# Turning the non-rotary queries of a latent attention on VectorE instead of TensorE, and moving the score products three tiles later

## The reference, cut to what matters

```python
q = (rms_norm(c_q, norm_cq) @ w_uq).reshape(B, S, MLA_HEADS, QK_NOPE + QK_ROPE)     # 128 + 64
q = jnp.concatenate([q[..., :QK_NOPE], apply_rope(q[..., QK_NOPE:], cos, sin)], axis=-1)
kv = (rms_norm(c_kv, norm_ckv) @ w_ukv).reshape(B, S, MLA_HEADS, QK_NOPE + V_HEAD)
...
s = jnp.einsum('bqhd,bkhd->bhqk', q[:, q0:kend], k[:, :kend]).astype(jnp.float32) * scale
p = jax.nn.softmax(jnp.where(mask, s, NEG_INF), axis=-1).astype(v.dtype)
outs.append(jnp.einsum('bhqk,bkhd->bqhd', p, v[:, :kend]))
```

## Time and profile before

| | |
|---|---|
| three runs | 1658.45 (median), 1657.43, 1869.51 us |
| the profiled execution | 1656.32 us, its span 1654.5 us |
| PE busy | 1645.2 us, 99% |
| DVE busy | 1156.0 us, 70% |
| ACT busy | 818.3 us, 49% |
| loads from HBM | 306.89 MB, 187 GB/s over the span |

### The profile page before, as it was taken

How to read it: one execution, slowest core, us unless ns; L and a number is a source line. 1 busy time by engine, 2 the same in 40 slices (tenths; PEclk the granted TensorE clock), 3 DMA queues, 4 the chain that set the end, 5 groups by cost and what they waited for, 6 DMA issues and landing times.

```text
span 1654.5 us, 23302 instructions
## 1 busy us (share of the span) xinstructions
PE 1645.2 (99%) x7752; PEld 1377.5 (83%) x7752; DVE 1156.0 (70%) x1528; ACT 818.3 (49%) x1044; POOL 109.7 (7%) x154
## 2 busy tenths in 40 slices
PE   9999999999999999999999999999999999999998
PEld 8888888888888888888888888888888888888886
DVE  5678877778988777885568766666666666654454
ACT  7556545555544544555555544444444444344343
POOL 3100111120000000120001100000000000000000
PEclk9999999999999999999999999999999999999999
DMA  7875655556566675554446666666666666565564
GB/s 238 250 205 171 181 163 146 167 160 186 162 190 204 199 231 169 200 196 155 145 132 193 198 193 196 195 190 192 192 194 183 190 203 194 195 219 180 186 211 137
DMA packets 161404, 309.81 MB, mean 187 GB/s; under 512 B 10272, under 2 KB 16928, under 8 KB 161088
## 3 DMA queue, kind: packets, MB, share of 16 engines
q1 hardware_dynamic: 159152, 302.03, 59.6%
q0 software_dynamic: 1488, 6.42, 1.1%
q10 hardware_dynamic: 704, 0.58, 0.1%
HBM read 306.89 MB, written 2.10 MB: 187 GB/s over the span
## 4 chain that ended last, share of the span: by engine, by line
PE 98%; ACT 1%; issue 1%; DMA 0%; DVE 0%; POOL 0%; POOLq 0%; ACTq 0%; SPq 0%; DVEq 0%
PE acc L374 30%; PE acc L376 30%; PE acc L375 30%; PE tp L386 1%; PE sc L527 1%; PE acc L603 1%; PE acc L605 1%; PE acc L604 1%; PE ov L508 0%; PE sc L522 0%; PE sc L497 0%; DMA raw<-in_w_in_dram 0%; PE ov L404 0%; PE acc L574 0%; PE acc L585 0%
## 5 line engine op out<-in xcount | busy, mean ns | idle before, releaser
L1339 DVE TENSOR_TENSOR w_lo<-raw,w_hi 128x1024 fp32r<-128x1024 f32 (+3 forms) x591 | 719.1, 1222 | 382.9 <-ACT w_hi L821 375.2
L821 ACT ACTIVATE w_hi<-raw 128x1024 fp32r<-128x1024 f32 (+3 forms) x591 | 605.7, 1027 | 753.8 <-PE acc L376 722.9
L374 PE MATMUL acc<-w_hi,crossT 128*128 128x512 f32 x832 | 324.8, 390 | 0.1
L375 PE MATMUL acc<-w_lo,crossT 128*128 128x512 f32 x832 | 323.9, 389 | 0.0
L376 PE MATMUL acc<-w_hi,crossT 128*128 128x512 f32 x832 | 323.9, 389 | 0.0
L374 PE MATMUL acc<-w_hi,mixT 128*128 128x512 f32 x732 | 289.1, 395 | 0.2
L376 PE MATMUL acc<-w_hi,mixT 128*128 128x512 f32 x732 | 285.2, 390 | 0.0
L375 PE MATMUL acc<-w_lo,mixT 128*128 128x512 f32 x732 | 285.1, 389 | 0.0
L374 PEld LDWEIGHTS acc<-w_hi,crossT 128*128 128x128 f32 x832 | 156.2, 188 | 33.0 <-ACTq L1072 0.5
L376 PEld LDWEIGHTS acc<-w_hi,crossT 128*128 128x128 f32 x832 | 156.2, 188 | 32.6
L375 PEld LDWEIGHTS acc<-w_lo,crossT 128*128 128x128 f32 x832 | 156.2, 188 | 31.9
(11 more groups left out here) (286 smaller groups left out, 1581.6 us busy)
## 6 DMA issues: line engine op xcount, KB each, us to landing
raw<-in_w_in_dram SPq DMA_DIRECT2D x104, 512.0 KB, 3.9
raw<-in_w_gate_dram SPq DMA_DIRECT2D x88, 512.0 KB, 3.9
raw<-in_w_up_dram SPq DMA_DIRECT2D x88, 512.0 KB, 3.7
raw<-in_w_down_dram SPq DMA_DIRECT2D x80, 512.0 KB, 4.6
raw<-in_w_kv_mem_dram SPq DMA_DIRECT2D x64, 512.0 KB, 3.7
raw<-in_w_o_dram SPq DMA_DIRECT2D x32, 512.0 KB, 4.4
raw<-in_w_q_mem_dram SPq DMA_DIRECT2D x32, 512.0 KB, 4.0
raw<-in_w_o_mem_dram SPq DMA_DIRECT2D x32, 512.0 KB, 4.1
```

The lines of the kernel that those rows point to most:

```text
L374: mm(o, lo, whi, start=first and k == 0, stop=False)
L375: mm(o, hi, wlo, start=False, stop=False)
L821: fn(w_hi[:, s, 0:width], raw[:, s, 0:width], ACT.Copy).then_inc(hi_done, 1)
L1339: V.tensor_tensor(w_lo[:, s, 0:width], raw[:, s, 0:width], w_hi[:, s, 0:width].bitcast(F32), ALU.subtract).then_inc(lo_done, 1)
```

## The change

The four transposes of the non-rotary queries leave PE. DVE does them as 16 instructions (`query_turn`), each of which transposes 32 x 32 squares of a 32-row band: for row band i and column band j the squares of both token blocks and both heads, 32 x 128 numbers. They stand between taps: squares 0 to 2 and 3 to 6 in steps 10 and 11 of the pair itself, 7 to 9, 10 to 12 and 13 to 15 in steps 0, 1 and 2 of the next pair (after the last pair: of the memory stage). DVE writes `qnT` itself, so ACT's copy of it goes. The two rotary transposes stay, now each in a bank of its own with its own copy on ACT. Values and scores on PE move from behind tile 3 to behind tile 6, masked scores on DVE from step 3 to 6, exponentials on ACT from step 4 to 7, the inverse of the row sums from step 7 to 8. The taps are shared out anew.

```diff
-            def queries_turned(p, q):
-
-                pe.wait_ge(q_ready, 2 * p + 2)
-                turn_group(q, 0, [q_tok[:, b, h, 0:NOPE] for h in range(2) for b in range(NB)])
+            def rotary_turned(p, q):
+
                 pe.wait_ge(rope_ready, p + 1)
-                turn_group(q, 1, [qr_tok[:, b, :, :].rearrange("p h d -> p (h d)") for b in range(NB)])
+                for b in range(NB):
+                    turn_group(q, b, [qr_tok[:, b, :, :].rearrange("p h d -> p (h d)")])
...
                 operand_ready(q)
+                pe.wait_ge(q_turned, p + 1)
                 pe.wait_ge(kv_ready, 2 * p + 2)
...
-                    queries_turned(i - 1, i + (Q_C - 1))
+                    rotary_turned(i - 1, i + (Q_C - 1))
                     if nth > 1:
                         probs_turn(i - 2)
-                if t == 3:
+                if t == 6:
                     if nth > 1:
                         values(i - 2, v_pair[parity], nth == 2)
                     scores(i - 1, i + (Q_C - 1), nth == 1)
...
-                fn(qnT[:, :, :].rearrange("p h t -> p (h t)"), tp[:, 0, :], ACT.Copy).then_inc(turned_out[0], 1)
-                act.wait_ge(turned, 2 * q + 2)
-                fn(qrT[:, :], tp[:, 1, 0:TOK], ACT.Copy).then_inc(turned_out[1], 1)
+                for b in range(NB):
+                    act.wait_ge(turned, 2 * q + (b + 1))
+                    fn(qrT[:, b * P:(b + 1) * P], tp[:, b, 0:P], ACT.Copy).then_inc(turned_out[b], 1)
...
-                if t == 4:
+                if t == 7:
                     exponentials(i - 1)
...
                         if not first:
-                            act.wait_ge(turned, 2 * i + (2 * Q_C - 1))
+                            act.wait_ge(q_turned, i)
                             act.wait_ge(rope_ready, i)
...
+            def query_turn(n):
+
+                i, j = n // 4, n % 4
+                src = q_tok[32 * i:32 * i + 32, :, :, 32 * j:32 * j + 32]
+                to = qnT[32 * j:32 * j + 32, :, :].rearrange("p h (b t) -> p b h t", b=NB)
+                ins = V.transpose(to[:, :, :, 32 * i:32 * i + 32], src)
+                if n == 15:
+                    ins.then_inc(q_turned, 1)
...
                     ins.then_inc(conv_step, 1)
+                    if turns:
+                        query_turn(turns.pop(0))
+                for n in turns:
+                    query_turn(n)
...
-                if t == 3:
+                if t == 6:
                     masked_scores(i - 1, nth == 1)
                 if t == 7:
                     if nth > 1:
                         gate_values(i - 2)
+                if t == 8:
                     row_inverse(i - 1, nth == 1)
...
-            share = [0, 0, 2, 3, 4, 6, 8, 10, 12, 14, 16, 18, EARLY_TAPS]
+            share = [0, 1, 3, 5, 8, 10, 12, 12, 13, 16, 18, 19, EARLY_TAPS]
...
-            share_last = [0, 3, 6, 7, 9, 12, 15, 18, 18, 18, 19, 19, EARLY_TAPS]
+            share_last = [0, 1, 3, 5, 9, 12, 15, 15, 16, 17, 18, 19, EARLY_TAPS]
+            turn_now = {0: (7, 10), 1: (10, 13), 2: (13, 16)}
+            turn_next = {10: (0, 3), 11: (3, 7)}
...
+                    turns = range(*turn_next.get(t, (0, 0)) if first or t > 9 else turn_now.get(t, (0, 0)))
+                    if t == 10:
+                        dve.wait_ge(q_ready, 2 * i + 2)
+                        if not first:
+                            dve.wait_ge(scores_ready, 2 * i)
...
-                late_taps(0, t, (0, 0, 1, 3, 6, 10, 14, 18, 22))
+                late_taps(0, t, (0, 1, 3, 5, 8, 12, 16, 18, 22), range(*turn_now.get(t, (0, 0))))
             for t in range(8):
                 split_lo(T_E + 8, t + 4)
+                if t == 0:
+                    row_inverse(PAIRS - 1, False)
```

More of the change, by code:

```diff
@@ L231, in program @@
         g_ready, u_turned, u_ready, tanh_done = (sem(n) for n in ("g_ready", "u_turned", "u_ready", "tanh_done"))
-        q_ready, kv_ready = sem("q_ready"), sem("kv_ready")
+        q_ready, q_turned, kv_ready = sem("q_ready"), sem("q_turned"), sem("kv_ready")
         rope_step, rope_ready = sem("rope_step"), sem("rope_ready")
@@ L965, in _, with rotary_out @@
                             fn(sqT[:, 2 * g:2 * g + 2, :], mem_k[:, 2 * g:2 * g + 2, :], ACT.Square).then_inc(sq_done, 1)
-            def queries_out(p, q, first):
-                act.wait_ge(turned, 2 * q + 1)
+            def rotary_out(p, q, first):
                 if not first:
                     act.wait_ge(scores_ready, 2 * p)
-                fn(qnT[:, :, :].rearrange("p h t -> p (h t)"), tp[:, 0, :], ACT.Copy).then_inc(turned_out[0], 1)
-                act.wait_ge(turned, 2 * q + 2)
-                fn(qrT[:, :], tp[:, 1, 0:TOK], ACT.Copy).then_inc(turned_out[1], 1)
+                for b in range(NB):
+                    act.wait_ge(turned, 2 * q + (b + 1))
+                    fn(qrT[:, b * P:(b + 1) * P], tp[:, b, 0:P], ACT.Copy).then_inc(turned_out[b], 1)
             def probs_evicted(p, first):
@@ L995, in attention @@
                 if t == 1:
-                    queries_out(i - 1, i + (Q_C - 1), nth == 1)
+                    rotary_out(i - 1, i + (Q_C - 1), nth == 1)
                     if nth > 1:
                         probs_evicted(i - 2, nth == 2)
-                if t == 4:
+                if t == 7:
                     exponentials(i - 1)
@@ L1462, in _, with taps @@
                         u_turn(t, c - 1)
-            def taps(j, w0, w1, before):
+            def query_turn(n):
[5 more added lines that the diff above has]
+                    ins.then_inc(q_turned, 1)
+            def taps(j, w0, w1, before, turns=()):
+                turns = list(turns)
                 for w in range(w0, w1):
@@ L1572, in gate_and_pair @@
                     at = share_first if first else share_last if last else share
+                    turns = range(*turn_next.get(t, (0, 0)) if first or t > 9 else turn_now.get(t, (0, 0)))
[3 more added lines that the diff above has]
+                            dve.wait_ge(scores_ready, 2 * i)
                     if at[t + 1] > at[t]:
-                        taps(i, at[t], at[t + 1], i * EARLY_TAPS + at[t])
+                        taps(i, at[t], at[t + 1], i * EARLY_TAPS + at[t], turns)
             gate_and_pair(0, 0)
@@ L1584, in _, with late_taps @@
             after_c = CT * EARLY_TAPS
-            def late_taps(c, t, at=(0, 3, 6, 9, 12, 15, 18, 21, 22)):
+            def late_taps(c, t, at=(0, 3, 6, 9, 12, 15, 18, 21, 22), turns=()):
+                turns = list(turns)
                 order = [(half, EARLY_TAPS + w) for half in range(2) for w in range(LATE)]
@@ L1590, in late_taps @@
                     half, w = order[n]
-                    taps(c * 2 + half, w, w + 1, c * (2 * LATE) + (after_c + n))
+                    taps(c * 2 + half, w, w + 1, c * (2 * LATE) + (after_c + n), turns[:1])
+                    turns = turns[1:]
+                for n in turns:
+                    query_turn(n)
             def key_turns(lo, hi):
```

## The result

The changed kernel takes 1662.83 us, the median of seven runs (1661.84 to 1664.98), against 1657.79 for the one before; the ratio is 1.0033, with a 95% interval of 1.0024 to 1.0043. One slow run of the seven before (1869.51 us) is left out of the ratio. I had forecast 1664.8, slightly slower and within 2%. The profiled execution took 1661.84 us, 5.5 more than the one before, where my sum had +6.4.

What follows compares the result with a forecast made beforehand. The prediction took PE to bound the kernel (98% of the chain). Its terms, -3.4 + 4.9 + 0.6 + 4.3 = +6.4 us on 1656.32, gave 1662.7, plus 2.1 for the median: 1664.8 us; range 1656.5 to 1672.

Steps and rivals of the forecast that it cites:

- both places: PE would wait at the first key product in seven pairs and at the memory stage's tiles 3 to 6.
- What leaves PE: On PE, four non-rotary query transposes a pair go, 0.43 us a pair over eight pairs: -3.4 us.
- What a square costs: On DVE, each 32 x 128 transpose takes 0.32 us (0.22 to 0.44); sixteen make 5.1 us a pair.
- The price of a tap ahead of a square: On DVE, a tap followed by a square costs 0.50 us instead of 0.40; seven a pair add 0.7 us.
- The exponentials: On ACT, four exponentials delay the copy freeing the keys' bank; PE waits 0.7 us in seven pairs: +4.9 us.
- Late maxima in the second pair: In the second pair DVE ends its maxima late, so ACT's exponentials start late: +0.6 us.
- The memory stage: DVE makes operands 2 to 6 late, so PE waits, mostly at tiles 3 to 6: +4.3 us.
- What stays covered: In a middle pair DVE's splits stay ahead of PE, DVE idles about 0.8 us, loads come early enough: no cost.
- DVE becomes the bound: Rival: squares from about 0.37 us use up DVE's idle time in the pairs, delaying maxima and bank; 1674.4 us, 15%.
- The sum: For the whole kernel, -3.4 + 4.9 + 0.6 + 4.3 = +6.4 us on the profiled 1656.32 us: 1662.7.

Runs made afterwards that it cites:

- the run with 32: The changed kernel with every square done twice, 32 a pair, the second into a spare buffer: 1679.61 us, ratio 1.013.
- both edits: The changed kernel with the last pair's queries turned by TensorE and, inside the pairs, exponentials at ACT's step 10: 1654.47 us, 0.9985 of the kernel before.

## Why the prediction was right

It was right in sign, in size, and in both places. By its steps:

- **What leaves PE, -3.4 us.** A little more. With the exponentials at step 10 no wait is left in the pairs, and a middle pair takes 33.55 us (296.63 to 330.18) instead of 34.02 (297.50 to 331.52): 0.47 us a pair, 3.8 in eight.
- **What a square costs.** Taken as 0.30 us long by the growth of other instructions, and as 0.32 in the sum; measured 302 ns (the mean of 128, row below) and 0.31 from start to start. The price of a tap ahead of a square, 0.50 instead of 0.40, is there too: 410.43 to 410.94. Ahead of the first square, whose bands are both 0, it isn't (407.17 to 407.56). The 0.9 us by which the prediction says that its sum would be lower without this price is not worked out there; its seven taps at 0.10 us make 0.7.
- **The exponentials, +4.9 us.** The mechanism was right, the term too large: 4.0 us, 0.54 to 0.60 in each of the seven pairs instead of 0.7. I took 0.7 from the second pair, where the bank had next to no slack. In a middle pair of the kernel before, the copy ended at 263.22 and the keys started at 263.48, 0.26 us later; in the changed kernel, where PE waits for the copy, it is 0.09 (332.62 to 332.71). So some 0.2 us of slack was there, which those rows would have shown.
- **Late maxima in the second pair, +0.6.** Measured 0.3: ACT's exponentials began at 192.70, 0.27 us later than ACT was free.
- **The memory stage, +4.3 us.** Measured 4.5. VectorE's list from the split at 406.02 to the end of operand 6 at 424.59 + 0.87 took 19.4 us, the sum forecast. At tile 2, where I had 0.4 us, PE waited for 0.35; tiles 3 to 6 took 0.7 to 1.2 each.
- **What stays covered.** Right in result, wrong in size. I said that a middle pair lasts 33.80 us and that VectorE would idle 0.8 us there. The 33.80 was about the mean over the pairs; the second one, with less attention work, takes 32.0 (163.34 to 195.34). A middle pair took 34.02 before and 34.14 after (298.57 to 332.71), and VectorE idled 1.98 + 0.22 us. So the rival *DVE becomes the bound* was drawn too near: with room for 1.9 us it would have begun at squares of about 0.42 us (an estimate), not 0.37. The rival is real, as the run with 32 shows, and in the second and the last pair it begins before 24. One thing was wrong in result: the loads do not all come early enough, as the last section shows, though PE did not wait for it.
- **The sum.** +6.4 against +5.5 in the profiled executions: the bank 1.2 too much (4.9 + 0.6 against 4.3), the transposes' gain 0.4 too small, the stage 0.2 too little, and 0.4 lost before the first pair, which no edit explains. That makes +5.4. The median came out 2.0 us below the forecast, 0.9 by this sum and 1.1 because it lies 1.0 us above its profiled execution and not 2.1.

The row for the squares of the changed kernel, DVE by line and shape:

```profile
L1469 DVE STREAM_TRANSPOSE qnT<-q_tok 32x128 f32<-32x128 f32 x128 | 38.7, 302 | 2.5
```

## What to carry to other kernels

When work leaves the bounding engine, read from the trace what each moved piece stands in front of in its new place: here 3.8 us of transposes were won, and 4.3 lost because four exponentials moved in front of a copy that frees a bank, though ACT idles half of the time. A stage next door with a tighter deadline (operands made just in time) pays for the added load even where the stage it was meant for has room. A mean busy share of the bounding engine doesn't show such waits. The chain that ended last doesn't measure them either: PE's share of it is 97% with the exponentials moved, where the memory stage's waits are left, and 95% with both edits, where neither wait is. The view of waits names the places, and the distances from start to start give the price.

## What the runs showed that I had not expected

A load became late on every pair without costing anything. ACT waits for the second tile of the query weights; in the changed kernel:

```profile
ACT w_hi L821 <- DMA raw<-in_w_uq_dram: 19.5, 7, 3.8
```

In the kernel before no such wait is among the larger ones. SP issues that load (tile 9) only when VectorE has split tile 6, one tile later than for other loads (`ahead=t`, L320), and VectorE now comes to tile 6 with the squares before it. The squares are the cause: with one square a pair ACT waits there only in the first two pairs (5.9 us), the second of which still has its squares ahead; with 24 squares it waits eight times (31.2 us). ACT is late there by up to 3.8 us and makes it up before PE wants the tile: in the version with both edits, the fastest of all, ACT waits 21.8 us for it. A large total in the view of waits is no cost as long as PE has none.
